# VectorE's order in a two-layer RWKV-7 and attention trunk: where the second weight group's two sums stand in the chunk recurrence

## The reference

```python
def token_shift(z, mu):
    prev = jnp.pad(z[:, :-1], ((0, 0), (1, 0), (0, 0)))
    return z + (prev - z) * mu
...
    def step(state, inp):
        r_t, w_t, k_t, v_t, a_t, b_t = inp
        sa = jnp.einsum('bhij,bhj->bhi', state, a_t)
        state = (state * w_t[:, :, None, :] + sa[..., None] * b_t[:, :, None, :]
                 + v_t[..., None] * k_t[:, :, None, :])
        return state, jnp.einsum('bhij,bhj->bhi', state, r_t)
...
for i in range(DEPTH):
    h = rms_norm(x, norm_mix_pre[i])
    z = h @ w_comb                       # r, k, v, three loras; q, k, v of the attention
    z_rwkv = token_shift(z[..., :N_SHIFT], shift_mu[i])
    y_r, v_r = rwkv7_mix(z_rwkv, ...)    # 16 heads x 64: gates, wkv7_scan, group norm, bonus
    y_a = moba_attention(q, k, v)        # 8 heads x 128; at 256 tokens one causal block
    x = x + rms_norm(concat(y_r, y_a) @ w_out[i], norm_mix_post[i])
    m = square(relu(rms_norm(x, norm_mlp_pre[i]) @ w_up[i])) @ w_down[i]
    x = x + rms_norm(m, norm_mlp_post[i])
```

## Time and profile before

| | us |
|---|---|
| median of 3 runs | 2477.32 (2475.15 to 2478.72) |
| the profiled execution's own time | 2476.58 |
| its span in the trace | 2474.7 |
| PE busy | 2447.8 (99%) |
| VectorE busy | 1664.9 (67%) |
| ScalarE busy | 1278.2 (52%) |
| GpSimd busy | 129.7 (5%) |

### The profile page before, as it was taken

How to read it: one execution, slowest core, us unless ns; L and a number is a source line. 1 busy time by engine, 2 the same in 40 slices (tenths; PEclk the granted TensorE clock), 3 DMA queues, 4 the chain that set the end, 5 groups by cost and what they waited for, 6 DMA issues and landing times.

```text
span 2474.7 us, 47858 instructions
## 1 busy us (share of the span) xinstructions
PE 2447.8 (99%) x15931; PEld 2061.0 (83%) x15931; DVE 1664.9 (67%) x2729; ACT 1278.2 (52%) x2096; POOL 129.7 (5%) x186
## 2 busy tenths in 40 slices
PE   8999999999999999999999999999999999999998
PEld 7888888888888888888788888888888888888887
DVE  6778877576556566466578888875765565664665
ACT  6566656555344344344456566655543443443443
POOL 3000101000000000000011112110000000000000
PEclk9999999999999999999999999999999999999999
DMA  7544454555665555655554444445656656556554
GB/s 212 144 127 118 133 145 131 192 185 178 202 186 188 195 178 196 194 187 188 161 144 138 121 121 138 135 130 190 187 181 200 188 185 195 178 195 195 180 195 153
DMA packets 437964, 420.07 MB, mean 170 GB/s; under 512 B 19566, under 2 KB 352000, under 8 KB 437888
## 3 DMA queue, kind: packets, MB, share of 16 engines
q1 hardware_dynamic: 434240, 412.55, 53.3%
q0 software_dynamic: 3648, 6.52, 0.9%
HBM read 416.90 MB, written 2.10 MB: 169 GB/s over the span
## 4 chain that ended last, share of the span: by engine, by line
PE 98%; DVE 1%; ACT 0%; DMA 0%; SPq 0%; issue 0%; DVEq 0%
PE gemm_bank L550 33%; PE gemm_bank L551 18%; PE gemm_bank L577 12%; PE gemm_bank L578 12%; PE gemm_bank L579 12%; PE gemm_bank L553 2%; PE mix_banks L737 1%; PE mix_banks L744 1%; PE mix_banks L708 1%; PE mix_banks L779 1%; PE mix_banks L785 1%; PE mix_banks L602 1%; PE mix_banks L775 1%; PE mix_banks L784 1%; PE mix_banks L680 0%; PE mix_banks L678 0%
## 5 line engine op out<-in xcount | busy, mean ns | idle before, releaser
L1256 DVE TENSOR_TENSOR b_wlo<-b_raw,b_whi 128x1024 fp32r<-128x1024 f32 x777 | 943.2, 1224 | 539.3 <-ACT b_whi L943 538.6
L550 PE MATMUL gemm_bank<-b_hT,b_whi 128*128 128x512 f32 x3420 | 1245.8, 405 | 1.1 <-DVE b_hT L1308 1.1
L943 ACT ACTIVATE b_whi<-b_raw 128x1024 fp32r<-128x1024 f32 x777 | 812.6, 1057 | 648.9 <-PE gemm_bank L579 422.5
L551 PE MATMUL gemm_bank<-b_hT,b_wlo 128*128 128x256 f32 x3648 | 1008.9, 281 | 0.0
L550 PEld LDWEIGHTS gemm_bank<-b_hT,b_whi 128*128 128x128 f32 x3420 | 642.6, 188 | 149.7 <-issue 2.7
L551 PEld LDWEIGHTS gemm_bank<-b_hT,b_wlo 128*128 128x128 f32 x3648 | 688.9, 189 | 11.2
L577 PE MATMUL gemm_bank<-b_whi,b_mT 128*128 128x512 f32 x1280 | 501.7, 392 | 0.3
L578 PE MATMUL gemm_bank<-b_wlo,b_mT 128*128 128x512 f32 x1280 | 498.4, 389 | 0.0
L579 PE MATMUL gemm_bank<-b_whi,b_mT 128*128 128x512 f32 x1280 | 498.3, 389 | 0.0
L577 PEld LDWEIGHTS gemm_bank<-b_whi,b_mT 128*128 128x128 f32 x1280 | 240.3, 188 | 50.2 <-issue 1.1
L579 PEld LDWEIGHTS gemm_bank<-b_whi,b_mT 128*128 128x128 f32 x1280 | 240.2, 188 | 50.2
(11 more groups left out here) (234 smaller groups left out, 1743.8 us busy)
## 6 DMA issues: line engine op xcount, KB each, us to landing
b_raw<-in_w_up SPq DMA_DIRECT2D x256, 512.0 KB
b_raw<-in_w_down SPq DMA_DIRECT2D x256, 512.0 KB
b_raw<-in_w_in SPq DMA_DIRECT2D x384, 256.0 KB
b_raw<-in_w_out SPq DMA_DIRECT2D x60, 512.0 KB
b_raw<-in_w_in SPq DMA_DIRECT2D x8, 512.0 KB
b_xt<-in_x SPq DMA_DIRECT2D x8, 256.0 KB, 5.7
b_raw<-in_w_out SPq DMA_DIRECT2D x8, 256.0 KB
out<-b_xt SPq DMA_DIRECT2D x8, 256.0 KB, 2.4
```

What stands on the lines that cost most here:

```text
L550: mm(bank[b0 + b][:, :], whi[r][:, cols], pair, start=first, stop=False)
L551: m = mm(bank[b0 + b][:, 0:SEQ], wlo[r][:, cols], act[:, kt, 0, :], start=False, stop=False)
L943: f(whi[r][:, :], raw[r][:, :, :].rearrange("p a b -> p (a b)"), ACT.Copy).then_inc(hi_done, 1)
L1256: tt(wlo[r][:, :], flat(raw[r][:, :, :]), whi[r][:, :].bitcast(F32), ALU.subtract).then_inc(lo_done, 1)
```

## The change

Before, `finish(1)` stood at the end of the second chunk's part of VectorE's program (c == 1), behind the state. Now it stands in the third chunk's part (c == 2), behind `Rb` and the decay of the old state, and in front of `key_shift(…, 0)`.

```diff
                     if c == 2:
+                        finish(1)
                         if more:
                             key_shift(l, i + 1, n + 1, 0)
                         else:
                             step(7)
...
                             m.then_inc(e["s_out"], 1)
-                    if c == 1:
-                        finish(1)
                     if c == 2:
```

## The result

| | before | after |
|---|---|---|
| median of 11 runs, us | 2476.23 (2475.15 to 2478.72) | 2482.68 (2479.69 to 2484.63) |
| ratio, 95% interval | | 1.0025 [1.0017, 1.0032] |
| span of the profiled execution, us | 2474.7 | 2482.4 |

The change made the kernel slower by 6.45 us, by its interval by 4.2 to 7.9 us (2476.23 times 0.0017 and 0.0032). The median of before that the prediction started from, 2477.32, came from the first three of these eleven runs.

The account below looks back on a forecast made before the run. PE, holding 98% of the chain that ended last, was taken to bound the kernel. 14 turns by 0.38 us are 5.3 us over the median of 2477.32, so 2482.6 us, range 2478.5 to 2485.5.

Parts of the forecast that it names:

- What it removes: PE's L779 load in the third chunk: its 0.27 us wait for VectorE's `Rb` goes, worth at most 3.9 us.
- What it puts later: Chain of sums, GpSimd's differences, key shift, state and PE's L775: the state comes 0.38 us later in each turn.
- The two steps on which I had chosen between bounds: Sums start at the decay's end (overlapped: 0.11 cheaper); the shift waits for GpSimd's second difference (no lock: 0.2 us smaller).
- The lock: VectorE instruction with two SBUF inputs and GpSimd instruction reading SBUF exclude each other; without it, 0.2 us less a turn.
- What stands behind: All that follows the state or PE's L775 moves by the same 0.38 us; nothing takes the shift up.
- The full gain: Rival: L779's wait goes and nothing takes its place; gain of the whole 3.9 us, 2473.4 us; chance 0.05.
- the point that I gave for it: GpSimd's start at 238.62 or sooner, from which the wait would go with nothing in its place.
- The shift did not get ahead of the difference: Rival: key shift runs before GpSimd's second difference, takes 0.47; state 0.17 later, 2.4 us in all, 2479.7; chance 0.07.
- the sums did not overlap the decay: Rival: VectorE's sums start before the decay ends; 0.27 a turn, 3.8 us in all, 2481.1 us; chance 0.16.
- the state did not wait for the end of the shift: Rival: VectorE's state starts only behind the key shift; 0.48 a turn, 6.7 us in all, 2484.0 us; chance 0.17.

Follow-up runs that it names:

- the first experiment: The change, with the key shift put behind the third chunk's state and the shift of r behind the two sums of y: 2473.70 us, run again 2474.21 us.
- the run with three more: The kernel before, with three more instructions like the key shift behind it, written to tiles that nothing reads then: 2483.48 us, ratio 1.0028.

## Why the prediction was right

The forecast was 2482.6 us and the median is 2482.68, but part of that nearness is chance: against the 2476.23 of eleven runs the loss is 6.45 us, where I had 5.3 against 2477.32. The interval of 4.2 to 7.9 us contains 5.3, and in the turns, where the loss is made, it is 5.43. I had given slower by over 0.2% a chance of 0.46; the ratio is 1.0025, but its interval begins at 1.0017, so the runs don't settle on which side of that bound the change lies.

*What it removes.* L779's wait for `Rb` went as said, and the first experiment shows what it is worth when nothing takes its place: 2.6 to 3.1 us in the turns, of the 3.9 that I named as the most (some 0.2 a turn, not 0.27).

*What it puts later.* From R's start, predicted and measured: sums 1.09 and 1.09, GpSimd 1.92 and 1.93, end of the shift 3.38 and 3.39, state 3.31 and 3.32, L775 3.96 and 3.96. The two steps on which I had chosen between bounds went as chosen: the sums began only at the decay's end (239.77 and 0.29, 240.09), and the shift took 0.69, ending 0.28 behind GpSimd's second difference (242.11). The lock of the Trainium skill, SBUF — State Buffer, section on who interferes with whom, agrees with the run that holds that difference back: without it the shift takes 0.48. That run shows that the overlap costs; that the shift stands still for all of it rests on where it ends, 0.27 to 0.28 behind the difference in the earlier trace rows, in the earlier trace rows and in the changed kernel.

*What stands behind.* I had said that nothing takes the late state up, without a row that showed it. The two runs with added work show that little is: the third instruction adds 0.40 and costs 0.37 a turn.

*The rivals.* The full gain does not come, since GpSimd starts 0.66 past the point that I gave for it (238.62 is 1.27 behind R's start; it was 1.93). The shift did not get ahead of the difference, the sums did not overlap the decay, and the state did not wait for the end of the shift (it starts 0.07 before it). The last was in part luck: I took the 0.07 from two shifts in the earlier trace rows, neither of which reads a bank, while the state reads one, and what that can change came out only in the experiments (last section).

*What is left.* Two sizes are a little off. A turn grew by 0.36 in layer 0 and 0.42 in layer 1, where L775 moved by 0.38 or 0.39 in both; seven turns of layer 1 differ by 0.44 us in the two profiles of the first experiment, so this is no more than scatter. And the median moved by about 1 us more than the turns. The rest of the span varies by 2.8 us among the ten profiles and by 2.0 between the two of one kernel, so I put this down to scatter too; that is likely, but not shown.

## What to carry to other kernels

An instruction that waits for another engine should not stand ahead of one that a chain waits for, unless its answer is sure to be there: here two sums were moved by 1.2 us to save a wait of 0.27, and the wait that they feed took the chain with it. Before moving work out of the way, follow who else waits for its result and where that answer is wanted in the same engine's order. The wait was worth removing, but only together with the consumer: with the key shift behind the state the same move gains 0.1%.

## What was not expected of the hardware

How soon the state followed its predecessor on VectorE went, in these runs, with the partition at which the last instruction that read a bank of PSUM began, even if others that read no bank stood between. In the changed kernel the state (from partition 0 on) starts 0.07 before the end of the shift, and the last bank read ahead of it was that of the sums, from partition 0. With the second difference held back the order is the same, and the state starts 0.08 before the end of a shift that nothing lengthens (240.56 and 0.48, 240.96). In the run with three more, the last bank read was `Rb`'s, from partition 64, and the state starts 0.02 after the end of its predecessor (242.64, 242.66), though the decay, the key shift and the three added ones, none of which reads a bank, stand between. This fits the model of the Trainium skill, VectorE: DVE Perf Modes, section on two Vector instructions with no wait between them, which the prediction used for the sums alone; no run changes the partition by itself. It is worth 0.09 us a turn here, and I had taken the state's start from another place of the trace, without seeing that the order of the bank reads may decide it.
